# Delta rule of a two-block layer on raw keys and queries: norms as factors per token, output norm by token

## What is computed

```
q = _l2norm(q) * (128 ** -0.5);  k = _l2norm(k)      # _l2norm(x) = x * rsqrt(sum(x*x) + EPS)
kb = k * beta
L = strict_lower((kb @ k.T) * exp(gc_i - gc_j))
u, w = solve(I + L, [v * beta, kb * exp(gc)])
a_qk = lower((q @ k.T) * exp(gc_i - gc_j))
qg = q * exp(gc);  kd = k * exp(g_last - gc);  S = 0
per chunk:  v_new = u - w @ S
            o = qg @ S + a_qk @ v_new
            S = S * exp(g_last) + kd.T @ v_new
out = _rmsnorm(o, o_norm) * silu(z)                  # _rmsnorm(o) = o * rsqrt(mean(o*o) + EPS) * o_norm
```

## Time and profile before

| | |
|---|---|
| median of 3 runs | 907.74 us (906.91 to 910.39) |
| the profiled execution, its own time | 907.85 us |
| its span, first to last instruction | 906.1 us |
| TensorE, VectorE, ScalarE, GpSimd busy | 879.6, 637.2, 504.2, 70.6 us |
| granted TensorE clock, mean over the span | 0.990 |

### The profile page before, as it was taken

The page is one execution under the profiler, slowest core; times in us unless marked ns, Lnnn a source line. Parts: engine busy times, 40 slices in busy tenths (PEclk is TensorE's granted clock), DMA queues, the critical chain, the costliest instruction groups (busy, mean ns, idle before and its releaser), DMA issues.

```text
span 906.1 us, 15149 instructions
## 1 busy us (share of the span) xinstructions
PE 879.6 (97%) x6082; PEld 807.9 (89%) x6082; DVE 637.2 (70%) x1126; ACT 504.2 (56%) x792; POOL 70.6 (8%) x77
## 2 busy tenths in 40 slices
PE   6989999999999999999998999999999999999997
PEld 6979999999989999999996989999999777778885
DVE  6797987978877666666668896757556545766665
ACT  6555777755478665565567764425435424354543
POOL 0200002001020111111112003000000000000000
PEclk9999999999999999999999999999999999999999
DMA  9438543557445655555553546432332322446541
GB/s 338 164 131 293 161 140 118 172 177 302 141 165 194 222 185 187 187 183 186 189 185 123 181 164 222 140 112 99 117 110 97 111 99 74 139 159 211 190 161 47
DMA packets 40446, 148.96 MB, mean 164 GB/s; under 512 B 4506, under 2 KB 4664, under 8 KB 39736
## 3 DMA queue, kind: packets, MB, share of 16 engines
q1 hardware_dynamic: 40376, 147.99, 48.4%
HBM read 146.90 MB, written 1.08 MB: 163 GB/s over the span
## 4 chain that ended last, share of the span: by engine, by line
PE 85%; DVE 9%; ACT 3%; issue 1%; DMA 1%; SPq 0%; DVEq 0%; ACTq 0%
PE bank L604 37%; PE bank L599 16%; PE bank L601 15%; PE bank L600 15%; DVE t_wl L1704 3%; DVE t_arena L1719 2%; PE bank L607 2%; DVE t_arena L1709 1%; ACT t_wh L1222 1%; ACT t_hh L1227 1%; DVE t_sm L1716 1%; DVE t_x L1719 1%; ACT t_arena L1227 1%; DMA t_x<-in_xin 1%; ACT L1227 0%
## 5 line engine op out<-in xcount | busy, mean ns | idle before, releaser
L1704 DVE TENSOR_TENSOR t_wl<-t_raw,t_wh 128x1024 fp32r<-128x1024 f32 x260 | 316.9, 1228 | 117.9 <-ACT t_wh L1222 117.2
L599 PE MATMUL bank<-t_hh,t_wh 128*128 128x256 f32 x1240 | 360.1, 290 | 6.3 <-DVE t_wl L1704 2.5
L601 PE MATMUL bank<-t_hh,t_wl 128*128 128x256 f32 x1240 | 352.0, 284 | 0.0
L600 PE MATMUL bank<-t_hl,t_wh 128*128 128x256 f32 x1240 | 351.9, 284 | 0.0
L1222 ACT ACTIVATE t_wh<-t_raw 128x1024 fp32r<-128x1024 f32 x260 | 272.7, 1058 | 128.6 <-PE bank L601 69.3
L599 PEld LDWEIGHTS bank<-t_hh,t_wh 128*128 128x128 f32 x1240 | 238.7, 193 | 10.8 <-issue 6.1
L600 PEld LDWEIGHTS bank<-t_hl,t_wh 128*128 128x128 f32 x1240 | 238.9, 193 | 0.8
L601 PEld LDWEIGHTS bank<-t_hh,t_wl 128*128 128x128 f32 x1240 | 238.7, 193 | 0.0
L604 PE MATMUL bank<-t_wh,t_br 128*128 128x512 f32 x384 | 123.6, 392 | 0.2 <-POOL t_br L2383 0.2
L1719 DVE SCALAR_TENSOR_TENSOR t_arena<-bank,t_par,t_arena 128x255 f32<-128x255 f32 (+1 forms) x180 | 73.5, 473 | 40.5 <-ACT t_arena L1227 40.5
L604 PEld LDWEIGHTS bank<-t_wh,t_br 128*128 128x128 f32 x384 | 72.1, 188 | 16.7 <-issue 1.8
(11 more groups left out here) (138 smaller groups left out, 857.8 us busy)
## 6 DMA issues: line engine op xcount, KB each, us to landing
t_raw<-in_ws SPq DMA_DIRECT2D x260, 512.0 KB, 4.0
t_br<-decay SPq DMA_DIRECT2D x1, 2048.0 KB, 9.0
t_arena<-in_post SPq DMA_DIRECT2D x3, 512.0 KB, 5.3
t_arena<-gates SPq DMA_DIRECT2D x1, 1536.0 KB, 10.0
t_x<-in_xin SPq DMA_DIRECT2D x4, 256.0 KB, 6.0
t_bd<-in_bd SPq DMA_DIRECT2D x1, 1024.0 KB, 11.9
t_x<-in_xtok SPq DMA_DIRECT2D x1, 1024.0 KB, 5.9
t_arena<-in_mem SPq DMA_DIRECT2D x1, 1024.0 KB, 8.2
```

Source lines behind the costliest of these rows:

```text
L599: e.matmul(o, wh, xh, start=first, stop=False, skip_group_check=True)
L600: e.matmul(o, wh, xl, start=False, stop=False, skip_group_check=True)
L601: return e.matmul(o, wl, xh, start=False, stop=last, skip_group_check=True)
L1704: e.tensor_tensor(WL[q % NS][:, :], RAW[q % NR][:, :], WH[q % NS][:, :].bitcast(F), SUB).then_inc(*lo.now(q))
```

## The change

The delta rule now works on unnormalized keys and queries.

- **Keys.** `kt0` and `kt1` are transposed first, at ticks 161 and 162. ScalarE sums their squares by token while it reads them from PSUM (`head_squares`, 8 instructions with an accumulator, into `KSUM`). VectorE writes `KBE` from the raw transposes, makes the reciprocal root r of 8 columns (`newton`), and from it r*r (`KINV`) and the factors of `VB` (`VBS`) and `KT` (`KTS`). The factor r*r also enters the products of `kk`, as the scalar of a three-operand instruction that replaces a two-operand one.
- **Queries.** Only q is squared (`QSQ`), and summed by 8 column sums. A common factor of a token's query cancels in the output norm except for its EPS, so the sum becomes that EPS (`QEPS`). `QSQ` lies where `ET` is written later, so GpSimd's first instruction on `ET` now also waits for `nq`.
- **Rows.** `row0` to `row3`, `no`, `orow0` and `orow1` are gone, with the VectorE products that read them.
- **Order.** The banks go round as kt0, kt1, nq, vt0, vt1, so `vt0` waits until VectorE has written `KT` from kt0's bank.
- **kk** is two products with 256 moving columns per head in place of four with 128.
- **Output.** `o{c}` comes with tokens on partitions: stationary q (128x64) and moving S (128 columns), stationary `ET` (64x64) and moving v_new. ScalarE sums its squares by token; at tick 206 VectorE makes the reciprocal root and scales; at tick 208 TensorE turns the result back (`ot0`, `ot1`, four transposes each), and one instruction per pair of heads applies gain and gate.

```diff
-DN_SEQ = [("nq", "D")] + [(f"row{i}", "D") for i in range(4)] + [("kt0", "D"), ("vt0", "D"), ("kt1", "D"), ("vt1", "D")]
+DN_SEQ = [("kt0", "D"), ("kt1", "D"), ("nq", "D"), ("vt0", "D"), ("vt1", "D")]
...
-DN_SEQ += [("no", "D"), ("orow0", "D"), ("orow1", "D")]
+DN_SEQ += [("ot0", "D"), ("ot1", "D")]
...
@@ TensorE, dn_lane
+                for hf in range(2):
+                    yield from walk.until(161 + hf)
+                    e.wait_ge(*a_silu.of("dnq3"))
+                    turn(f"kt{hf}", [k_[:, h, 128 * hf:128 * hf + 128] for h in range(4)])
                 yield from walk.until(163)
...
+                e.wait_ge(*a_dn.of("sq"))
+                for h in range(4):
+                    m = column_sums(dn_bank("nq"), 2 * h, [QSQ[:, h, :]], h == 0, h == 3)
                 m.then_inc(*p_dn.now("nq"))
...
                 for hf in range(2):
...
+                    yield from walk.until(164 + 2 * hf)
                     e.wait_ge(*a_silu.of("dnq5"))
                     turn(f"vt{hf}", [v_[:, h, 128 * hf:128 * hf + 128] for h in range(4)])
...
+                        m = mm(two(3 + h % 3)[:, hf, :].rearrange("p (w e) -> p w e", w=2), k_[:, h, sl], QKV[:, h:h + 5:4, sl])
...
-                            mm(o, S[:, h, :], QKV[:, h, 64 * c:64 * c + 64], h == 0, False)
-                        m = mm(o, U[r, hf, h, :], ET[r, hf, h, r], c == 0 and h == 0, True)
+                            mm(o, QKV[:, h, 64 * c:64 * c + 64], S[:, h, :], h == 0, False)
+                        m = mm(o, ET[r, hf, h, r], U[r, hf, h, :], c == 0 and h == 0, True)
...
@@ VectorE, dn_lane
+                yield from walk.until(162)
+                ts(HDNN, pc("dnn"), 0.5, MUL).then_inc(*d_dn.now("hdnn"))
+                e.wait_ge(*d_rw.of("bge"))
+                for hf in range(2):
+                    e.wait_ge(*a_dn.of("ksq", hf))
+                    by_token(KBE[:, hf, :, :], heads(v_of(f"kt{hf}")), bge[:, hf, :]).then_inc(*d_dn.now("kbe", hf))
                 yield from walk.until(163)
...
+                e.wait_ge(*p_dn.of("nq"))
+                ts(QEPS.rearrange("p (f h) -> p f h", f=2), PB[v_of("nq")][:, 0:8].rearrange("p (h f) -> p f h", f=2),
+                   128 * EPS, MUL, 128 * EPS * EPS, ADD).then_inc(*d_dn.now("nq"))
+                ts(NW[:, 1, 0:8], KSUM, EPS, ADD).then_inc(*d_rs.now("dnk", "v"))
+                newton("dnk", NW, 8)
+                kr, kv = (NW[:, i, 0:8].rearrange("p (a b) -> p a b", a=2) for i in range(2))
+                e.wait_ge(*d_rs.of("dnk"))
+                stt(VBS, kv, -2.0, kr, MUL, MUL).then_inc(*d_dn.now("norm"))
+                tt(KINV, kr, kr, MUL).then_inc(*d_dn.now("kinv"))
...
                 for hf in range(2):
...
+                    by_token(KT[:, hf, :, :], heads(v_of(f"kt{hf}")), KTS[:, hf, :]).then_inc(*d_dn.now(f"kt{hf}"))
...
+                yield from walk.until(206)
+                e.wait_ge(*a_dn.of("osq", 1))
+                e.wait_ge(*d_dn.of("nq"))
+                stt(NW[:, 1, 0:8], OSUM, 1.0 / 128, QEPS, MUL, ADD).then_inc(*d_rs.now("dno", "v"))
+                newton("dno", NW, 8)
+                e.wait_ge(*d_rs.of("dno"))
+                for hf in range(2):
+                    by_token(ONT[:, hf, :, :], OTK[:, hf, :, :], NW[:, 0, 4 * hf:4 * hf + 4]).then_inc(*d_dn.now("on", hf))
...
```

More of the change, by code:

```diff
@@ L815, in bank @@
                     n = DN_AT[name]
-                    if n >= 3 and DN_SEQ[n - 3][0] not in ("kt1", "vt0", "vt1"):
+                    if n >= 3 and DN_SEQ[n - 3][0] not in ("vt0", "vt1"):
                         e.wait_ge(*dn_emptied(DN_SEQ[n - 3][0]))
@@ L955, in dn_lane @@
                         yield
-                    bank(f"orow{i}")
-                    for j in range(2):
-                        m = spread(dn_bank(f"orow{i}"), T * j, 4 * i + 2 * j, j == 0)
-                    m.then_inc(*p_dn.now(f"orow{i}"))
+                    e.wait_ge(*d_dn.of("on", 1))
+                    turn(f"ot{i}", [ONT[:, n % 2, 2 * i + n // 2, :] for n in range(4)])
                 yield
@@ L1054, in turn_merged @@
                 if hf == 0:
-                    e.wait_ge(*d_dn.of("orow1"))
+                    e.wait_ge(*d_dn.of("y", 1))
                 for q in range(2):
@@ L1397, in dn_lane, with head_squares @@
             def dn_lane():
+                def head_squares(src, o, sums, hf, done):
+                    for h in range(4):
+                        m = e.activation(o[:, hf, h, :], src[:, h, :], ACT.Square, accum_out=sums[:, 4 * hf + h:4 * hf + h + 1])
+                    m.then_inc(*done)
                 def empty(name, o):
@@ L2039, in update @@
                     tt(Q[:, hf, :, :], Q[:, hf, :, :], heads(v_of(name)), op).then_inc(*d_dn.now(name))
-                yield from walk.until(163)
-                rsqrt("dnq", NW, v_of("nq"), 16, 1, p_dn.of("nq"))
-                for i in range(4):
-                    yield from walk.until(164 + i // 2)
-                    qk = QKV[:, 2 * i:2 * i + 2, :]
-                    e.wait_ge(*p_dn.of(f"row{i}"))
-                    stt(qk, qk, 128.0 ** -0.5 if i < 2 else 1.0, two(v_of(f"row{i}")), MUL, MUL).then_inc(*d_dn.now(f"row{i}"))
@@ L2056, in dn_lane @@
+                e.wait_ge(*d_dn.of("kinv"))
+                tt(KTS, KINV, dc[:, 3, :, 4:8], MUL).then_inc(*d_dn.now("kts"))
+                e.wait_ge(*d_dn.of("kts"))
+                for hf in range(2):
+                    by_token(KT[:, hf, :, :], heads(v_of(f"kt{hf}")), KTS[:, hf, :]).then_inc(*d_dn.now(f"kt{hf}"))
+                for hf in range(2):
+                    yield from walk.until(164 + 2 * hf)
                     e.wait_ge(*p_dn.of(f"vt{hf}"))
-                    tt(VB[:, hf, :, :], heads(v_of(f"vt{hf}")), dc[:, 0, hf, 0:4].unsqueeze(2).to_broadcast([P, 4, 128]),
-                       MUL).then_inc(*d_dn.now(f"vt{hf}"))
+                    e.wait_ge(*d_dn.of("vbs"))
+                    by_token(VB[:, hf, :, :], heads(v_of(f"vt{hf}")), VBS[:, hf, :]).then_inc(*d_dn.now(f"vt{hf}"))
```

95 lines of the change are left out of this document (35 added, 60 removed).

## The result

The changed kernel took 902.31 us (median of four executions, 900.39 to 903.69), the kernel before 908.1 beside it: a ratio of 0.9932, with a 95% interval of 0.9905 to 0.9959. That is 5.8 us less by the medians, and 6.2 by the ratio, which compares means. The profiled execution was the quickest of the four, 900.39 us with a span of 898.6, so the two profiles lie 7.5 us apart. The prediction was 902.0.

The account below looks back on a forecast made before the run. TensorE's list was taken as the bound, busy 879.6 of 906.1 us; -7.9 - 1.9 - 3.1 + 0 + 4.1 + 1.2 + 1.7 = -5.9 us from 907.85 gave 902.0 us, with an 8-in-10 range of 897.5 to 907.0.

Parts of the forecast that it names:

- Work that leaves the list: On TensorE: halved nq, dropped rows and no, and output rows turned into transpositions save 7.9 us; kk counts nothing.
- Old losses: On TensorE behind the column sums of nq: the low-clock stretch and the wait for the root go, 1.9 us less.
- Clock behind the output products: On TensorE behind o1 and o2: both low-clock stretches go, 1.55 us each, 3.1 us less.
- The output products themselves: TensorE's output blocks: no change in time; bounds for three blocks 2.2 us less and 1.6 more.
- New wait 1: TensorE at vt0 waits for VectorE's 18 small instructions at 0.35 us and the KT scaling: 4.1 us more.
- Clock after it: TensorE behind the wait at vt0: one fall of the clock, partly inside the wait, 1.2 us more; ends nothing and 3.1.
- the single stretch that was named as a sign: On TensorE's timeline: a low clock once, around 561 to 566 us.
- New wait 2: TensorE's mask matmul at tick 207 waits for VectorE's output norm and two scalings: 1.7 us more; bounds nothing and 2.2.
- 1 (the clock still falls): Behind TensorE's output products the clock still falls, 3.1 us come back: 905.1 us; chance 0.17.
- 2 (the chain is quick because GpSimd is not what stretches it): VectorE's chain ahead of vt0: wait only 1.5 us, too short for a clock fall: 898.2 us; chance 0.18.
- 3 (each of the 13 two-input instructions waits for a whole GpSimd instruction): VectorE's chain ahead of vt0 takes 8.2 us, making the wait 5.4 us: 903.3 us; chance 0.10.
- 4 (the clock stays low for long): TensorE behind the wait at vt0 stays at 1.2 GHz for 18 us, costing 8.1 us: 908.9 us; chance 0.05.

Follow-up runs that it names:

- experiment 9: Changed kernel with value transposes a tick later, output norm behind the sliding-window product, and the query norm's 16 column sums made twice: 898.00 us, ratio 0.9894.
- experiment 7: Changed kernel with value transposes a tick later, output norm behind the sliding-window product, and output products in their old form: 896.97 us, ratio 0.9874.
- norms_only: Kernel before plus only the key and query norm half of the change, output products and output norm left old: 906.17 us, ratio 0.9974.
- experiment 4: Changed kernel with GpSimd's decay instructions held until VectorE has written KT: 900.08 us, ratio 0.9912.
- experiment 2: Changed kernel with VectorE's output norm one lane call later in tick 206, behind the sliding-window product: 899.49 us, ratio 0.9906.

## Why the prediction was right, point by point

The time was right to 0.3 us, and the mechanism was the one it named. Most terms hold. That the sum came so near is luck: one wait was taken 1.3 us too long and the clock's terms were off the other way.

- **Work that leaves the list, 7.9 us.** Right. `nq` lasts 1.84 us as 16 records and the next product starts 1.70 behind it (553.88), `ot0` and `ot1` are transposition blocks of 0.60 us. `kk` at nothing: from one head to the next block of the stream it is 4.19 us (579.69 to 583.88) where it was 4.21 (585.11 to 589.32).
- **Old losses, 1.9 us.** Right in kind, and tested: with 16 column sums and no long wait the clock did not fall in five profiles, with 32 it fell in three of three (experiment 9 has one of them).
- **Clock behind the output products, 3.1 us.** Right in direction: none in 27 blocks of the new form. The size was read off one profile, which had two stretches. Over nine old blocks of three kernels it is 4 falls, so 1.3 for three blocks, about 2 us, and experiment 7 lost 0.8 to 1.4 us. For the kernel before itself two may still be the usual number, since most of its executions have one mean clock; so the term lies between 2.0 and 3.1.
- **The output products themselves, 0.** The block went from 2.87 to 2.96 us and from 4.39 (`norms_only`, at the full clock) to 4.48 us to the next `vn` block: 0.3 us for the three. Inside the bounds of -2.2 and +1.6.
- **New wait 1, 4.1 us.** The wait and its cause were right, its size was not: 2.76 us. The term that was mis-sized is the price of 0.35 us for a small instruction beside GpSimd, taken from the 13 of before. These 18 took 0.27 each. The 13 read 16 columns and each waited for its forerunner; the 18 have 8 columns, and some don't wait. GpSimd's part is 0.09 us each (experiment 4), against 0.15 for the 13 (4.50 less 2.60, by 13). Which of the two differences makes it was not tried. The prediction's two prices differ in this as well: its 13 at 0.35 have 16 columns and its 13 at 0.20 have 8, so their ratio is not GpSimd's part alone. And the rows that it names for the one-input instructions, the first and last of each group, show no stretch (0.17 and 0.18); in the trace it lies in those between, 0.30 and 0.39 us for a single one.
- **Clock after it, 1.2 us.** I had one fall in mind, a part of it inside the wait. What the profiles show is a chance: 2 of 4 executions, once double. As a mean it comes to 1.1 us by the profiles and to 0.5 by the mean clocks, and of the four profiles only that of `norms_only` had the single stretch that was named as a sign (from 559.75). The profiled execution had none, which is a part of why its span lies 7.5 us under that of before and the medians only 5.8.
- **New wait 2, 1.7 us.** Right: 1.64 us. What the sum did not have is the low stretch behind it, 1.5 us in three profiles of five, 0.9 as a mean.
- **The rivals.** 1 (the clock still falls) is refuted by the 27 blocks. 2 (the chain is quick because GpSimd is not what stretches it) named 898.2, under every execution measured (the lowest is 900.39), and its reason is refuted: with GpSimd away the chain took 1.67 us less. That a wait of 1.5 us is too short for a fall of the clock, as it assumes, is not shown either: behind the mask matmul, the clock fell in three of five profiles after a wait of 1.6. 3 (each of the 13 two-input instructions waits for a whole GpSimd instruction) wanted a wait of 5.4 us, and 2.76 were measured. The rule of the Trainium skill that stands beside it (SBUF — State Buffer, "Who interferes with whom") has the direction right here, but a two-input pair of 0.37 us became 0.63, with GpSimd instructions of 0.4 to 0.6 us beside it (half a pair of the rows above); a wait for a whole one before each of the two would have made it over 1, as an estimate from these rows. 4 (the clock stays low for long) did not come; the longest low time behind a wait was the two stretches of experiment 2. Its counter-argument overlooks one low stretch of the trace before, which begins at 902 and lasts to the end; TensorE has no work there.

By the sum: work -7.9, old losses -1.9, output products about -2.0 and +0.3, wait 1 and its clock +2.8 +1.1, wait 2 and its clock +1.6 +0.9. That is -5.1, with -5.8 measured (-6.2 by the ratio) and an interval of some 2.5 us to either side. The clock's share may be larger than this sum has it (-1.5, with the old fall behind the column sums): the mean clock rose from 0.9904 over 19 executions to 0.9948 over nine, 4 us at full speed, of which about 1 is the shorter stretch at the end. Wait 1 was 1.3 too dear, and the clock at two other places 2.0 too cheap.

## What to carry to other kernels

A chain of tiny instructions is a wait as long as the chain if its consumer's slot stands right behind the producer's. Before replacing matmul work by small VectorE steps, count the steps, price them with the neighbour engine at work, and move the consumer a slot back: here two small moves in the order were worth more (6.8 us) than the change itself (5.8). And a stretch at the low clock seen in one profile is a sample: read the place in several executions, or take its mean granted clock, before it goes into a sum at full price.

## What the runs showed of the hardware that I had not expected

- The form of a product went with the clock at an equal number of records. 16 records with 128 stationary and 64 moving columns were followed by 1.2 GHz in 4 of 9 blocks, 16 records with 64 stationary and 128 moving columns in 0 of 27, at nearly the same duration (2.87 and 2.96 us). Both sides of the product changed at once, so which of them matters was not tried.
- The same wait, 2.75 to 2.77 us at the same place, left the clock at 2.4 GHz in two profiles of the changed kernel and took it to 1.2 GHz for two stretches in another kernel that differs only 200 us later.
- Small VectorE instructions of 8 columns cost 0.18 us each alone and 0.27 beside GpSimd, one-input ones among them (one went from 0.17 to 0.31). Nothing in the kernel's own order shows this price; only the timeline with both engines does.
- ScalarE's squares with a sum per token start 0.25 us apart with 128 columns (the four of `kt0` at 548.48, 548.73, 548.98, 549.23), so eight of them took 2.2 us beside TensorE's path.
